# A two-block transformer step with product-key experts: block products further ahead, gates in one buffer, rings of six, look-ups spread differently

## What is computed

```python
q = (xb @ w_q).reshape(PEER_BLOCK, PEER_HEADS, 2, PEER_HALF)
s = jnp.einsum('thpd,hpnd->thpn', q, sub_keys).astype(jnp.float32)
s_top, i_top = lax.top_k(s, PEER_TOPK)
cand = s_top[:, :, 0, :, None] + s_top[:, :, 1, None, :]
cand_idx = i_top[:, :, 0, :, None] * PEER_N_KEYS + i_top[:, :, 1, None, :]
...
best, pos = lax.top_k(cand, PEER_TOPK)
expert = jnp.take_along_axis(cand_idx, pos, axis=-1)
g = jax.nn.softmax(best, axis=-1)
act = jax.nn.gelu(jnp.einsum('td,thkd->thk', xb, u[expert]), approximate=False)
return jnp.einsum('thk,thkd->td', (g * act).astype(xb.dtype), v[expert])
```

## Time and profile before

| | us |
|---|---|
| Median of three runs (3739.09 to 3744.2) | 3740.57 |
| Profiled execution, its own time | 3747.75 |
| Span of its trace | 3746.0 |
| PE busy, share of the span | 91% |
| DVE busy, share of the span | 64% |
| TensorE clock, mean granted share | 0.922 |

### The profile page before, as it was taken

One profiled execution on the slowest core, in us unless ns is written; L12 is line 12 of the kernel. 1 busy time (PEld: TensorE's weight loads), 2 busy tenths in 40 slices (PEclk: granted clock), 3 DMA queues, 4 the chain that ended last, 5 costly groups with the idle time before them and its releaser, 6 DMA issues.

```text
span 3746.0 us, 44437 instructions
## 1 busy us (share of the span) xinstructions
PE 3400.7 (91%) x16120; PEld 2188.2 (58%) x16120; DVE 2393.4 (64%) x4969; ACT 1254.1 (33%) x3215; POOL 1306.5 (35%) x1028
## 2 busy tenths in 40 slices
PE   6976979889999999998959999796899999999987
PEld 3434644367777777765524455343777777777654
DVE  1048543777788888776751222348968889877667
ACT  2122112144555545520011123111455555455100
POOL 0000000003566676676700000000055666766675
PEclk9988679969999999999979976898699999999998
DMA  3211122307999999999941110130199999999998
GB/s 113 90 67 62 54 82 102 112 24 280 353 380 399 375 396 406 382 407 409 409 176 68 34 57 1 34 124 23 41 359 362 396 397 361 409 406 383 408 409 347
DMA packets 271690, 908.07 MB, mean 242 GB/s; under 512 B 30536, under 2 KB 31192, under 8 KB 270960
## 3 DMA queue, kind: packets, MB, share of 16 engines
q0 software_dynamic: 147456, 536.94, 36.8%
q1 hardware_dynamic: 124016, 368.29, 26.2%
HBM read 900.90 MB, written 4.22 MB: 242 GB/s over the span
## 4 chain that ended last, share of the span: by engine, by line
PE 76%; DVE 9%; DMA 7%; POOL 4%; issue 2%; ACT 1%; SPq 0%; DVEq 0%; POOLq 0%
PE psum L595 18%; PE psum L605 17%; PE psum L631 10%; PE psum L529 8%; PE psum L582 6%; POOL w L1690 4%; PE psum L754 3%; DMA w<-in_peer_up,tmp 2%; PE psum L538 2%; DMA w<-in_peer_u,tmp 2%; PE psum L795 2%; PE psum L815 2%; PE psum L695 2%; PE psum L685 2%; DMA w<-in_peer_v,tmp 1%
## 5 line engine op out<-in xcount | busy, mean ns | idle before, releaser
L595 PE MATMUL psum<-hT,mod 128*128 128x256 f32 x4096 | 955.1, 387 | 30.0 <-ACT hT L1006 29.2
L595 PEld LDWEIGHTS psum<-hT,mod 128*128 128x128 f32 x4096 | 779.5, 194 | 167.8 <-issue 69.0
L1545 DVE SCALAR_TENSOR_TENSOR tmp<-w,small,tmp 128x1024 f32<-128x1024 f32 x508 | 652.7, 1285 | 123.5 <-DMA w<-in_peer_up,tmp 55.6
L1690 POOL DMA_INDIRECT w<-in_peer_u,tmp x256 | 334.3, 1306 | 1031.4 <-DVEq L1422 874.0
L1527 DVE CUSTOM_DVE_ANT_0 w<-w,hn 128x1024 f32<-128x1024 f32 x512 | 608.2, 1222 | 112.6 <-DMA w<-in_peer_u,tmp 57.2
L1690 POOL DMA_INDIRECT w<-in_peer_down,tmp x256 | 332.4, 1298 | 986.9 <-DVEq L1422 827.3
L1016 ACT ACTIVATE levels<-key_numbers,hT 128x128 bf16<-128x128 f32 x1664 | 528.3, 390 | 315.5 <-PE psum L631 315.4
L605 PE MATMUL psum<-rows,hT 128*128 128x512 f32 x1024 | 460.5, 592 | 0.5 <-DVE hT L1484 0.4
L631 PEld LDWEIGHTS psum<-x,levels 128*128 128x128 bf16 x6144 | 382.2, 118 | 121.5 <-issue 110.6
L631 PE MATMUL psum<-x,levels 128*128 128x32 bf16 x6144 | 401.3, 238 | 19.6 <-DVE x L1464 13.2
L1690 POOL DMA_INDIRECT w<-in_peer_v,tmp x256 | 322.3, 1259 | 199.1 <-DVE tmp L1545 127.5
(11 more groups left out here) (282 smaller groups left out, 3094.7 us busy)
## 6 DMA issues: line engine op xcount, KB each, us to landing
mod<-in_uT SPq DMA_DIRECT2D x256, 512.0 KB, 6.7
rows<-in_peer_v SPq DMA_DIRECT2D x64, 512.0 KB, 6.8
rows<-in_peer_up SPq DMA_DIRECT2D x64, 512.0 KB, 6.9
w<-in_w_in SPq DMA_DIRECT2D x14, 2048.0 KB, 7.8
w<-in_ada_w SPq DMA_DIRECT2D x12, 2048.0 KB, 7.9
srow<-in_peer_v SPq DMA_DIRECT2D x32, 512.0 KB
tmp<-in_peer_v SPq DMA_DIRECT2D x32, 512.0 KB, 6.8
srow<-in_peer_up SPq DMA_DIRECT2D x32, 512.0 KB
```

The lines of the kernel that those rows point to most:

```text
L595: last = nc.tensor.matmul(ps[4 + e % 2][:, 0:ND], ub[e % UV][:, k, :], hT[:, k, ND:SEQ], start=k == 0, stop=k == KC - 1)
L1545: last = stt(y, vr[b], c8[g % 2][:, b:b + 1], y, ALU.mult, ALU.add)
L1690: nc.gpsimd.indirect_dma_start(ring[b], None, table, bass.IndirectOffsetOnAxis(idx[:, c:c + 1], 0))\
```

## The change

- PE does the first products of 16 blocks ahead instead of 4 (`AHEAD`), and does them between the batches of quarter 0. In the loop it computes `first_product(e + 16)`. Twenty buffers (`ZG`) hold the products that wait. The first layer starts the batches with one product done, the second with four.
- The gates keep one 32 KB buffer. Quarter q + 1 is copied into the places that quarter q's blocks have just left, 16 tokens per two blocks, with the layout changing between quarters; the batches in the loop come at two per block.
- The freed space holds the twenty buffers and two more slots for each of the rings of rows (`ROWS = 6`). Units still have four rows.
- The look-up is split: heads 0 to 5 right after the third pair's top 16 (`numbers`), heads 6 and 7 at the end; sums of the one-hot products are taken by halving adds instead of a reduction. In the queries, tile 0 is done for two pairs instead of three. The rest of tile 0's choice is done between the batches of quarter 0 (41 pieces with `first_pieces`), not in the loop.
- `units_due` starts at block 1 instead of 5: `(e - 1) * 128 / 125`. DVE makes two of three hit batches of quarter 0 instead of three of four.

```diff
-AHEAD = 4
+AHEAD = 16
+ZG = 20
+RING = 4
+ROWS = 6
 HITS = 4
+EARLY_HEADS = 6
...
-    return q > 0 or n % 4 == 0
+    return q > 0 or n % 3 == 0
...
-EARLY_PIECES = 3 * PAIR_PIECES
-TILE_STEPS = 5
...
+EARLY_PIECES = 2 * PAIR_PIECES
+TILE_STEPS = 1
+
+
+def due(j, ahead, most, per=1):
+
+    return 0 if j < 0 else min(most, int(j * per) + ahead)
+
+
+def blocks_before(layer, n):
+
+    first = 1 if layer == 0 else 4
+    return first + (AHEAD - first) * n // BATCHES
...
-        gates = [part(big, 32 - 32 * b, 32) for b in range(2)]
...
+        ur = [part(w_, 4 * b, 4) for b in range(4)] + [part(big, 4 * b, 4) for b in range(2)]
+        vr = [part(w_, 16 + 4 * b, 4) for b in range(4)] + [part(big, 8 + 4 * b, 4) for b in range(2)]
+        gates_ = part(big, 32, 32)
+        gates = [gates_.rearrange("p (a i j) -> p a j i", a=QA, i=8), gates_.rearrange("p (j i a) -> p a j i", a=QA, i=8)]
...
                 for n in range(BATCHES):
                     gates_of_batch(layer, 0, n)
+                    for e in range(blocks_before(layer, n), blocks_before(layer, n + 1)):
+                        first_product(layer, e)
...
-                    for n in range(batches_due(q, j - 1), batches_due(q, j)):
-                        gates_of_batch(layer, q + 1, n)
+                    if q + 1 < QUARTERS:
+                        for n in range(due(j - 1, 4, BATCHES, 2), due(j, 4, BATCHES, 2)):
+                            gates_of_batch(layer, q + 1, n)
...
+                if q:
+                    act.wait_ge(blk_ready, layer * NKEY + (q - 1) * QA + 2 * m + 2)
...
+                    for k in (8, 4, 2):
+                        step(tt(oh[:, 0:k * slots], oh[:, 0:k * slots], oh[:, k * slots:2 * k * slots], ALU.add))
+                    step(tt(dst[t % 2 if t in DENSE else 0][:, c], oh[:, 0:slots], oh[:, slots:2 * slots], ALU.add))
...
-                    for t in DENSE + (0,) if p < 3 else DENSE:
+                    for t in DENSE + (0,) if p < 2 else DENSE:
                         for _ in head_experts(t, p):
                             pass
...
+                    if p == 2:
+                        for t in DENSE:
+                            for _ in numbers(t, 0, EARLY_HEADS):
+                                pass
+                for t in DENSE:
+                    for _ in last_numbers_and_gates(t):
                         pass
```

More of the change, by code:

```diff
@@ L222, in build @@
         nibT = hT[:, 2, 0:ND]
-        zg = [hT[:, 3 + n, 0:ND] for n in range(4)]
+        zg = [hT[:, 3 + n, 0:ND] for n in range(4)] + [part(big, 16 + n, 1) for n in range(ZG - 4)]
         iaT = hT[:, 7, 0:ND]
@@ L270, in build @@
         top_ = sb("chosen", 1024)
-        ia, ib = [part(top_, 0.5 * n, 0.5) for n in range(2)]
+        ia = [part(top_, 0, 0.5), part(big, 46, 0.5)]
+        ib = [part(top_, 0.5, 0.5), part(big, 46.5, 0.5)]
         bv = [part(big, 9, 0.5)] + [part(top_, 1 + 0.5 * (b % 2), 0.5) for b in (0, 1, 0)]
@@ L454, in _ @@
             set_x_aside(0)
-            for e in range(AHEAD):
+            for e in range(UV):
                 first_block(0, e)
@@ L735, in _ @@
             modulation(9)
+            modulation(10)
             turn_picks(0, 0)
-            modulation(10)
             modulation(11)
-            pe.wait_ge(sc_used, 16)
-            for e in range(AHEAD):
-                first_product(0, e)
             turn_picks(0, 1)
+            first_product(0, 0)
             dense_experts(0)
@@ L830, in _ @@
             turn_picks(1, 0)
+            turn_picks(1, 1)
             first_product(1, 2)
             first_product(1, 3)
-            turn_picks(1, 1)
             dense_experts(1)
@@ L1071, in _ @@
             modulation(8)
+            modulation(9)
             gate_exp(DENSE[0])
-            modulation(9)
+            modulation(10)
+            gate_exp(DENSE[1])
             copy_picks(0, 0)
-            modulation(10)
             modulation(11)
-            for e in range(3):
-                block_gelu(0, e)
-            gate_exp(DENSE[1])
             copy_picks(0, 1)
+            block_gelu(0, 0)
             dense_acts(0)
@@ L1413, in numbers_and_gates, with last_numbers_and_gates @@
+            def last_numbers_and_gates(t):
+                step = picks
+                for g, v, h in gate_parts(t):
+                    last = tt(g, v, v[:, :, 0:1].to_broadcast([P, h.stop - h.start, TOPK]), ALU.subtract)
+                last.then_inc(dve_to_act, 1)
+                yield from numbers(t, EARLY_HEADS, NH)
                 if t in GATHERED:
-                    step(stt(idf, ia, float(NKEY), ib, ALU.mult, ALU.add))
+                    step(stt(idf, ia[0], float(NKEY), ib[0], ALU.mult, ALU.add))
@@ L1490, in peer @@
                         second_keys(n)
-                early = [EARLY_PIECES, 0]
-                chooser = [tile_experts(t, early[t] // PAIR_PIECES) for t in GATHERED]
+                    for _ in range(first_pieces(n - 1), first_pieces(n)):
+                        next(chooser[0])
                 weigh_block(0)
```

241 lines of the change are left out of this document (122 added, 119 removed).

## The result

The changed kernel takes 3775.44 us (median of 4 runs, 3770.83 to 3783.7), beside 3739.83 us for the kernel before on the same chip: a ratio of 1.0096, 95% interval 1.0076 to 1.0116. It is slower by 1%. The forecast was 3775, with 0.68 on slower. The profiled execution took 3776.6 us of its own, with a span of 3774.7, 28.7 more than the span before. That is less than the 35.6 us between the medians: the profiled execution before was 7.2 us above its kernel's median, the one after 1.2.

A forecast was written before the change was run, and what follows sets the result against it. PE was taken to bound the first 96 blocks, DMA the last 32. 26 + 32.5 + 18 - 42 = 34.5 us on the profiled 3747.75 gave 3782, forecast as 3775 since runs stand 7.2 us lower; range 3728 to 3825.

The forecast's parts named there:

- What bounds the kernel: In each expert layer, the first 96 blocks are bound by PE and the last 32 by DMA, at 405 to 411 GB/s.
- the signs asked for: Marks of being right, among them last stages of 220 us at 409 GB/s with PE idle for over 50 us.
- Term 1: Ahead of the gates: the batches begin 24 us earlier in the first layer and 7.5 us earlier in the second.
- its 50.7 us: Ahead of the first layer's gates: DVE work said to stand in the 24 us before the fourth pair's scores.
- Terms 2 and 3: Between the gates: added products start block 0's second product 26 and 32.5 us later; the low clock costs 18 us, both layers.
- the rival that was given 0.10: Between the gates: DVE bounds or starts look-ups late, PE waits some 15 us per layer, 3805 us; chance 0.1.
- Term 4: Last 32 blocks: fewer bytes left to load, 87.6 MB, save 21 us per layer, 42 in all.
- What costs nothing: In the loop: strided gate reads in `weigh_block`, copies in place, queue order and early rows are hidden, at no cost.
- Rows in flight: Last stage: eight slots, not bandwidth, were the limit; twelve save 25 us less per layer to 196, 3725 us; chance 0.13.
- The clock that stays low: Between the gates: all 27 products pay 2.6 us, 70 instead of 18, 3827 us; chance 0.13.
- that stays up: Between the gates: the clock stays up, so the 18 us fall away, 3757 us; chance 0.17.

The follow-up runs named there:

- The rows sooner: The change with GpSimd's rows asked for at a quicker pace, 104 of 128 groups due by block 96 instead of 96: 3713.7 us, ratio 0.9933.
- Four ahead: The change with first products four blocks ahead instead of sixteen, everything else of it kept: 3760.26 us, ratio 1.0063 against the kernel before.
- the first expectation behind it: Expectation for the change with first products four ahead instead of sixteen: 3727 us expected, 3760.26 us measured.
- the second, 26 us out: Expectation for the change with first products eight ahead instead of sixteen: 3740 us expected, 3765.98 us measured.

## Why the prediction was right

**What bounds the kernel.** Right: the first 96 blocks by PE (811.4 of 811.4 us), the last stage by DMA (397 GB/s in all, and a third fewer slots cost it 2 and 9 us of some 220). The rows sooner showed both at once. Two of the signs asked for were not met: PE idles for 44.5 and 42.6 us of the last stages, not for over 50, and their rate is 397 and 398 GB/s over the stage, with 409 only in its steady part. The sum had used 398.

**Term 1, the gates start earlier.** -24.7 us (forecast -24) and, less the 9.1 us that layer 1 began late, -8.1 (-7.5). The size was right, but two of its parts were off and cancelled. DVE's list, from the third pair's scores to the last dense tile's softmax, took 65.0 us (693.29 to 758.33) for the 67.1 reckoned and began 1.1 us earlier. What follows it took 9.7 us for 7.2, since DVE waited 4.2 us for ACT's copy of the picks instead of 1.4. One reading in the prediction is wrong: of its 50.7 us, 14.7 are the fourth pair's own look-up, which can't start before its scores, so 35.9 stand in the 24. The 67.1 doesn't rest on it. (Two small sums are out by 0.3: 761.5 and what follows make 768.4, and 23.9 less 14 is 9.9.) The new look-up by its rows, in the change:

```profile
711.11 0.96 DVE L1420 TENSOR_TENSOR mod<-mod 128x1536 bf16<-128x1536 bf16 x1
712.10 0.96 DVE L1424 TENSOR_TENSOR mod<-mod 128x1536 bf16<-128x1536 bf16 x1
713.09 1.24 DVE L1426 TENSOR_TENSOR mod<-mod 128x768 bf16<-128x768 bf16 x3
714.37 0.26 DVE L1427 TENSOR_TENSOR chosen<-mod 128x96 f32<-128x96 bf16 x1
```

Two operations of 1536 at 0.96 each, and 1.5 us for the four adds, as reckoned; 10.2 us a tile for 10.6.

**Terms 2 and 3, products between the gates and the clock.** Together they had the second product of block 0 26 + 32.5 us later, and 18 for the clock: 76.5. Measured: 33.5 + 43.7 = 77.2. The granted clock was 0.91 and 0.87 in the two stretches, at the upper end of the 0.6 to 0.9 looked for. 5 of 15 products in layer 0 and 7 of 12 in layer 1 ran at the low level or partly so, each 1.5 to 2.4 us longer than 3.69: some 20 us for a forecast 18, more of them than the 7 it stood for, and each cheaper than 2.6. That number and price missed in opposite directions is luck.

The sum came out right, but one sentence of its reasoning did not stand: that work put between the gates costs its full length. It is so where DVE has little to do (37 us for twelve in layer 0, 42.6 in layer 1), and not beside the look-up (21 and 23.5). Four ahead, DVE's 82 us are the most work in the stretch (the rival that was given 0.10, which is false for sixteen ahead and mostly true for four), and on average about half of each product is covered. The forecast was safe since at sixteen ahead PE's 111 us outweigh DVE's 82 by far, which the prediction had worked out as 97 to 104 against 79; it did not ask what the stretch would be without the products. This is why the first expectation behind it missed by 33 us; in the second, 26 us out, the slower products at the low clock have a part.

**Term 4, the last stage.** 22.3 and 23.2 us less for a forecast 21 each: 87.17 MB in the DMA view for 87.6. The split between blocks ahead and rings was right too: four ahead leaves 232.4 us, 10 below the 242.1 before, for rings and pace; twelve blocks more ahead bring 12.6.

**What costs nothing.** True of the loop, and only there. `weigh_block` takes 0.605 us instead of 0.42, and in the first 96 blocks PE waits for nothing. Its waits for weighed blocks, 60.0 us on line 618, all lie in the last stages (28.7 and 31.3), where DVE comes to `weigh_block` behind rows that DMA has yet to bring. What the prediction did not price is ACT's copy of the gates into the new layout:

```profile
L1040 ACT ACTIVATE big<-psum 128x512 f32<-128x512 f32 x128 | 137.5, 1074 | 465.7 <-PE psum L644 465.7
```

It took 594 ns each in the kernel before. In the loop DVE waited 48.8 us for such copies at the three new quarters of layer 0, and PE not at all. Between the gates, with few products there and the look-up gone, PE's waits were all for ACT (12.7 us), which had the slower copies and the larger share of hit batches. Putting the share back brought about 10 us in all; what the copies cost there was not run by itself.

**The rivals.** Rows in flight (0.13): the last stages stayed at 397 and 398 GB/s with twelve slots, as with eight before. The clock that stays low (0.13) and that stays up (0.17): it flips, as the forecast had it.

**The number.** The sum of 34.5 us agrees with the 35.6 between the medians and with the 36.0 of the two layers. That 3775 came out within 0.5 us is luck: single executions of the change spread over 13 us.

## What to carry to other kernels

When two engines share a stretch, the price of an addition to one of them is not a number of its own: write down each engine's busy time in the stretch as it will be; the greatest is a lower bound. Here 12 products cost 37 us alone and 21 beside a look-up, which cost 16.6 alone and nothing beside them. The stretch of layer 0 took 2 to 5 us more than the greatest where PE had most by far (111.2 of 115.8, 113.4 of 115.6), and 10 to 19 more where the engines were closer (67.8 of 78.2, 81.9 of 94.8, 89.8 of 108.5), as they then wait for each other.

Before moving work of the engine that has most of the chain, total the bytes of the whole loop and its rate by stage: here one stage was bound by PE with DMA at 376 of 409 GB/s, the next by DMA, and an altered table of due times that moved bytes from the second to the first was worth 28 us on the kernel before, while the blocks ahead, the rings and the new order together cost 36.

If a stream later runs at its limit, look at when it starts: bytes not moved at the start come back at the end, even if every engine is busy in between. Here 8.1 MB fewer in the first 50 us, 20 us at 409 GB/s, went with a loop 22.5 us longer; no run altered the start alone.

## What the runs showed of the hardware

DMA kept 407 GB/s over 920 us (374.41 MB, most slices at 408 to 410) with PE busy for 756 of the first 761 us beside it. The 375 GB/s of the loop before was what the kernel asked for, no limit; and in the last stages of layer 0, before and after, no slice passed 411, but for one of 417 right behind one of 315.

The layout of a float32 operand changed an operation's time with the same number of elements. ACT's copy of 128x512 from PSUM went from 0.594 to 1.074 us when its writes, until then in runs of 16 elements, became single elements 128 bytes apart, and the multiplication of 256 elements by gates read at that stride from 0.42 to 0.605. The Trainium skill (SBUF — State Buffer, "Door 1: The DMA port swizzle") says that accesses which cross to a new 16-byte line each pay a penalty, so that four float32 values is how far a stride is free. The traces agree in direction, with 1.8 times for a strided write and 1.4 for one strided read of two; no run here varied the stride.
